# Splitting three of the four first w_ada groups, loading one whole group ahead of x, and scaling x's first blocks out of PSUM

## The reference

```python
sc = jax.nn.silu(c)                                   # c: 1 prompt row and 8 sampled rows
mod = sc @ w_ada + b_ada                              # 9 x 6144
sh1, s1, g1, sh2, s2, g2 = jnp.split(mod, 6, axis=-1)
h = rmsnorm(x, norm1_g) * (1 + s1) + sh1
z = h @ w_in                                          # 520 x 6144, then the three mixers, w_o, the experts
```

## Time and profile before

| | |
|---|---|
| median of three runs | 871.22 us (870.71 to 872.97) |
| the profiled execution | 873.34 us, of which the span of its instructions is 871.5 |
| TensorE matmul busy | 837.3 us, 96% of the span |
| VectorE busy | 686.0 us, 79% |
| ScalarE busy | 465.5 us, 53% |
| GpSimd busy | 77.0 us, 9% |
| mean granted TensorE clock | 0.988 |

### The profile page before, as it was taken

How to read it: one execution, slowest core, us unless ns; L and a number is a source line. 1 busy time by engine, 2 the same in 40 slices (tenths; PEclk the granted TensorE clock), 3 DMA queues, 4 the chain that set the end, 5 groups by cost and what they waited for, 6 DMA issues and landing times.

```text
span 871.5 us, 14885 instructions
## 1 busy us (share of the span) xinstructions
PE 837.3 (96%) x5035; PEld 699.3 (80%) x5035; DVE 686.0 (79%) x942; ACT 465.5 (53%) x556; POOL 77.0 (9%) x71
## 2 busy tenths in 40 slices
PE   7899999999999999999999889999999999999994
PEld 2589999989899999899777457888888888887851
DVE  0681638878798679599438879999989999899888
ACT  4552442343422221642222457888888888888852
POOL 0002000000000000230000001000100001003750
PEclk9889999999999999999999999999999999999998
DMA  9858545445443321123671579988896899999962
GB/s 329 276 166 277 200 126 170 138 151 164 148 152 118 97 80 66 55 74 123 237 251 73 175 275 390 393 313 317 312 400 219 322 398 400 400 399 397 359 196 98
DMA packets 90997, 201.24 MB, mean 231 GB/s; under 512 B 8792, under 2 KB 13400, under 8 KB 90918
## 3 DMA queue, kind: packets, MB, share of 16 engines
q1 hardware_dynamic: 78813, 165.25, 53.8%
q0 software_dynamic: 5136, 18.42, 6.0%
q10 hardware_dynamic: 7003, 16.95, 5.2%
HBM read 182.97 MB, written 18.35 MB: 231 GB/s over the span
## 4 chain that ended last, share of the span: by engine, by line
PE 81%; DVE 9%; DMA 3%; ACT 2%; issue 2%; SPq 1%; ACTq 1%; POOL 0%; POOLq 0%; DVEq 0%
PE ps L806 31%; PE ps L657 12%; PE ps L659 12%; PE ps L658 12%; PE ps L886 3%; DVE w_lo L1592 2%; PE ps L1001 2%; DMA region_a<-in_x_prompt_dram 2%; PE ps L1123 1%; PE ps L685 1%; PE ps L686 1%; PE ps L838 1%; ACT w_hi L1148 1%; DMA region_b<-h_rows,slot_idx 1%; PE ps L1036 1%
## 5 line engine op out<-in xcount | busy, mean ns | idle before, releaser
L1592 DVE TENSOR_TENSOR w_lo<-raw,w_hi 128x1024 fp32r<-128x1024 f32 x202 | 241.5, 1225 | 100.1 <-ACT w_hi L1148 98.3
L1148 ACT ACTIVATE w_hi<-raw 128x1024 fp32r<-128x1024 f32 x202 | 207.9, 1056 | 198.2 <-PE ps L806 150.6
L657 PE MATMUL ps<-w_hi,hT_hi 128*128 128x512 f32 (+1 forms) x512 | 205.6, 401 | 3.6 <-DVE w_lo L1592 1.4
L659 PE MATMUL ps<-w_hi,hT_lo 128*128 128x512 f32 (+1 forms) x512 | 202.1, 395 | 0.0
L658 PE MATMUL ps<-w_lo,hT_hi 128*128 128x512 f32 (+1 forms) x512 | 201.5, 393 | 0.0
L806 PE MATMUL ps<-hT_hi,w_hi 128*128 128x260 f32 x768 | 156.4, 285 | 1.9 <-ACT region_b L1242 1.1
L806 PE MATMUL ps<-hT_lo,w_hi 128*128 128x260 f32 x768 | 155.0, 283 | 0.0
L806 PE MATMUL ps<-hT_hi,w_lo 128*128 128x260 f32 x768 | 154.9, 283 | 0.0
L806 PEld LDWEIGHTS ps<-hT_hi,w_hi 128*128 128x128 f32 x768 | 118.8, 189 | 5.2 <-DVE w_lo L1592 3.9
L806 PEld LDWEIGHTS ps<-hT_lo,w_hi 128*128 128x128 f32 x768 | 119.4, 190 | 0.0
L806 PEld LDWEIGHTS ps<-hT_hi,w_lo 128*128 128x128 f32 x768 | 118.9, 189 | 0.0
(11 more groups left out here) (337 smaller groups left out, 838.6 us busy)
## 6 DMA issues: line engine op xcount, KB each, us to landing
raw<-in_exp_w_dram SPq DMA_DIRECT2D x96, 512.0 KB
region_a<-in_exp_w_dram SPq DMA_DIRECT2D x80, 512.0 KB
raw<-in_w_in_dram SPq DMA_DIRECT2D x48, 512.0 KB
raw<-in_w_ada_dram SPq DMA_DIRECT2D x30, 512.0 KB
expert_rows<-region_b ACTq DMA_DIRECT2D x17, 512.0 KB, 6.3
region_b<-in_exp_w_dram SPq DMA_DIRECT2D x16, 512.0 KB
region_b<-in_w_ada_dram SPq DMA_DIRECT2D x14, 512.0 KB, 8.1
expert_rows<-region_a POOLq DMA_DIRECT2D x8, 512.0 KB, 8.4
```

Of the source, the lines that this page charges most:

```text
L657: pe.matmul(out, pairs[0], moving[0], start=start, stop=False)
L659: return pe.matmul(out, pairs[1], moving[0], start=False, stop=stop)
L1148: act.activation(w_hi[:, split_slot(n), :], place, ACT.Copy).then_inc(hi_done, 1)
L1592: return dve.tensor_tensor(out, whole, first.bitcast(F32), ALU.subtract)
```

## The change

The first four w_ada groups are done as three split ones (0, 1 and 3) and one whole one (2); before, it was two and two. So twelve split quarters stand ahead of z 0 instead of eight (`N_HEAD`). SP loads group 0 (split quarters 0 to 3), the four whole quarters, then x, then the rest. TensorE starts with 32 identity transposes, products 0 to 3, the parameters, the four whole quarters, the turning of groups 0 and 2, and has more strings of identity transposes. ScalarE makes highs 0 to 3 and copies the whole group out before its squares of x, and scales x's tiles 2 and 3 itself. For blocks 0 to 3 of x ScalarE's copy to SBUF is gone: VectorE's `prompt_sum` reads PSUM, and ScalarE makes the high part from VectorE's sum. Blocks 4 to 7 go as before. All turning of mod now stands ahead of z 0. `z_quarter` becomes `z_part`, one call for each m, in the same order.

```diff
-G_NAT = 2
+G_WHOLE = 2
 G_HEAD = 4
 G_GAP = 2
-ITEMS = [("a", g) for g in range(G_NAT, G_HEAD)] + [("z", 0), ("z", 1)]
+HEAD_GROUPS = [g for g in range(G_HEAD) if g != G_WHOLE]
+ITEMS = [("a", g) for g in HEAD_GROUPS] + [("z", 0), ("z", 1)]
...
+N_NAT = 4
-N_HEAD = 4 * (G_HEAD - G_NAT)
+N_HEAD = 4 * len(HEAD_GROUPS)
+X_BANK = (2, 3, 6, 0, 2, 3, 6, 0)
...
@@ SP @@
-            for h in range(6):
-                native(h)
+            for n in range(4):
+                quarter(n)
+            for h in range(N_NAT):
+                sp.dma_start(native_place(h).rearrange("p (k n) -> p k n", k=2), ada_v[:, 2 * h:2 * h + 2, G_WHOLE * COLS:(G_WHOLE + 1) * COLS]).then_inc(nat_ready[h], 16)
             sp.dma_start(x_in[0:ND, 4, :], x_sample.rearrange("b t d -> (b t) d")).then_inc(x_landed[4], 16)
             for i in range(NP // P):
                 sp.dma_start(x_in[:, i, :], x_prompt[0, i * P:(i + 1) * P, :]).then_inc(x_landed[i], 16)
-            for h in range(6, 4 * G_NAT):
-                native(h)
-            for n in range(N_MIX):
+            for n in range(4, N_MIX):
...
@@ TensorE @@
-            pe.wait_ge(turned_out, 1)
-            for h in range(6):
-                native_quarter(h)
-            head_running(28)
-            for h in range(6, 4 * G_NAT):
-                native_quarter(h)
-            pe.wait_ge(xn_ready, NTILE)
-            for k in range(4):
-                turn_x(k, k)
-            pe.wait_ge(cT_split, 2)
-            ada_quarter(0, 4)
-            ada_quarter(1, 4)
-            for k in range(4, KD):
-                pe.wait_ge(xT_out, k - 3)
-                turn_x(k, k - 4)
-            ada_quarter(2, 4)
-            ada_quarter(3, 4)
-            pe.wait_ge(xT_out, KD)
-            turn_params()
-            ada_quarter(4, 7)
-            ada_quarter(5, 7)
-            pe.wait_ge(fold_ready, 1)
-            for g in range(3):
-                t = turn_mod(g, 0, 36 * g)
-            t.then_inc(modT_done, 1)
+            head_running(32)
+            pe.wait_ge(cT_split, 2)
+            for n in range(4):
+                ada_quarter(n, 4)
+            turn_params()
+            for h in range(N_NAT):
+                native_quarter(h)
+            pe.wait_ge(fold_ready, 1)
+            turn_mod(0, 1, 0)
+            head_running(8)
+            turn_mod(2, 1, 36).then_inc(modT_done, 1)
+            head_running(24)
+            for n in range(4, 6):
+                ada_quarter(n, 7)
+            pe.wait_ge(xn_ready, NTILE)
+            for k in range(2):
+                turn_x(k, X_BANK[k])
+            turn_sampled()
             ada_quarter(6, 7)
+            for k in range(2, 4):
+                turn_x(k, X_BANK[k])
             ada_quarter(7, 7)
+            for k in range(4, 6):
+                pe.wait_ge(hT_sum, k - 3)
+                turn_x(k, X_BANK[k])
+                ada_quarter(k + 4, 4)
+            for k in range(6, KD):
+                pe.wait_ge(hT_sum, k - 3)
+                turn_x(k, X_BANK[k])
+            ada_quarter(10, 4)
+            turn_mod(1, 7, 0)
+            ada_quarter(11, 4)
+            head_running(6, 1)
+            turn_mod(3, 7, 36).then_inc(modT_done, 1)
+            head_running(6, 1)
...
@@ ScalarE @@
-            native_out(0)
+            for n in range(4):
+                hi(n)
+            act.wait_ge(nat_used, N_NAT)
+            act.activation(mod[0:ND + 1, G_WHOLE * COLS:(G_WHOLE + 1) * COLS], ps[0:ND + 1, 5, :], ACT.Copy).then_inc(nat_out, 1)
             for n, i in enumerate((4, 0, 1, 2, 3)):
                 act.wait_ge(x_landed[i], 16)
...
             def input_prompt(k):
+                if k < 4:
+                    act.wait_ge(hT_sum, k + 1)
+                    act.activation(hT_hi[:, k, 0:NP], (tmp_a, tmp_b)[k % 2][:, 0:NP], ACT.Copy).then_inc(hT_hi_done, 1)
+                    return
...
+            for i in (2, 3):
+                act.wait_ge(x_rooted, 1)
+                act.activation(x_in[:, i, :], x_in[:, i, :], ACT.Copy, scale=sums[:, 3, i:i + 1]).then_inc(xn_ready, 1)
             hi(4)
             hi(5)
             input_sampled(0)
             input_prompt(0)
+            input_prompt(1)
+            hi(6)
+            input_prompt(2)
+            hi(7)
+            input_prompt(3)
             hi(8)
+            turned_x(4)
             hi(9)
+            for k in range(5, KD):
+                turned_x(k)
+            for n in range(10, 14):
+                hi(n)
             input_sampled(1)
...
@@ VectorE @@
+            for n in range(4):
+                lo(n)
+            mod_group(0)
+            params_out()
+            shift_out(0)
+            scale_out(0)
             mean_squares()
             norm_root()
-            for t in range(NTILE):
+            dve.wait_ge(shift_done, 1)
+            dve.sem_inc(x_rooted, 1)
+            for t in (4, 0, 1):
                 dve.tensor_scalar(x_in[0:rows(t), t, :], x_in[0:rows(t), t, :], sums[0:rows(t), 3, t:t + 1], None, ALU.mult).then_inc(xn_ready, 1)
+            lo(4)
             lo(5)
+            prompt_sum(0)
+            sampled_out()
             sampled_input(0)
+            prompt_sum(1)
             sampled_rest(0)
             prompt_rest(0)
+            lo(6)
+            prompt_rest(1)
+            prompt_sum(2)
+            lo(7)
+            mod_group(1)
+            prompt_sum(3)
+            prompt_rest(2)
             lo(8)
+            prompt_rest(3)
+            lo(9)
+            lo(10)
+            lo(11)
+            lo(12)
             mod_group(3)
+            shift_out(1)
             scale_out(1)
             sampled_input(1)
             prompt_sum(4)
             sampled_rest(1)
             prompt_rest(4)
+            lo(13)
...
```

More of the change, by code:

```diff
@@ L280, in trunk_step @@
         ld_x = sem("ld_x")
+        x_rooted = sem("x_rooted")
+        shift_done = sem("shift_done")
         x_landed = [sem(f"x_landed{i}") for i in range(NTILE)]
-        nat_ready = [sem(f"nat_ready{h}") for h in range(4 * G_NAT)]
+        nat_ready = [sem(f"nat_ready{h}") for h in range(4 * G_GAP)]
         apart_ready = [sem(f"apart_ready{n}") for n in range(N_APART)]
@@ L783, in z_quarter @@
                 hi, lo = split_weights(n, 2)
-                for m in range(4):
[L785 to L797, removed]
-                    for k in range(2):
-                        kk = 2 * q + k
-                        if g == 0 and m == 0:
-                            pe.wait_ge(hT_lo_done, kk + 2 + kk // 4)
-                        first, final = kk == 0, kk == KD - 1
-                        for w, x, start, stop in ((hi, hT_hi, first, False), (hi, hT_lo, False, False), (lo, hT_hi, False, final)):
-                            for h in range(2):
-                                mm = pe.matmul(ps[:, 2 * m + h, 0:HT], w[:, k, ms], x[:, kk, h * HT:(h + 1) * HT], start=start, stop=stop)
-                    if q == 3 and m < 3:
-                        mm.then_inc(z_done, 1)
@@ L810, in z_quarter @@
-                mm.then_inc(quarter_used, 1)
-            for i in range(G_HEAD - G_NAT, len(ITEMS)):
+                ms = slice(m * P, (m + 1) * P)
+                if q == 0:
+                    pe.wait_ge(set_free[m], g + 1)
+                    if m == 2 and ITEMS[n // 4 - 1][0] == "a":
+                        pe.wait_ge(mod_ready, SPLIT_GROUPS.index(ITEMS[n // 4 - 1][1]) + 1)
+                    elif m == 3 and g == 0:
+                        pe.wait_ge(scaleT_ready, 2)
+                for k in range(2):
+                    kk = 2 * q + k
+                    if g == 0 and m == 0:
+                        pe.wait_ge(hT_lo_done, kk + 2 + kk // 4)
+                    first, final = kk == 0, kk == KD - 1
+                    for w, x, start, stop in ((hi, hT_hi, first, False), (hi, hT_lo, False, False), (lo, hT_hi, False, final)):
+                        for h in range(2):
+                            mm = pe.matmul(ps[:, 2 * m + h, 0:HT], w[:, k, ms], x[:, kk, h * HT:(h + 1) * HT], start=start, stop=stop)
@@ L813, in _ @@
+                if m == 3:
+                    mm.then_inc(quarter_used, 1)
+                elif q == 3:
+                    mm.then_inc(z_done, 1)
+            pe.wait_ge(xT_out, KD // 2)
+            for q in range(4):
+                for m in range(4):
+                    z_part(0, q, m)
+            for i in range(len(HEAD_GROUPS) + 1, len(ITEMS)):
                 kind, g = ITEMS[i]
@@ L822, in _ @@
                     else:
-                        z_quarter(g, q)
+                        for m in range(4):
+                            z_part(g, q, m)
             unit = [0]
@@ L1212, in _ @@
                 input_prompt(k)
-            hi(10)
-            hi(11)
-            for n in range(N_HEAD + 4, N_HEAD + 7):
+            for n in range(N_HEAD + 2, N_HEAD + 7):
                 hi(n)
@@ L1227, in _ @@
             act.wait_ge(pads_ready, 1)
-            for i in range(G_HEAD - G_NAT, len(ITEMS)):
```

(7 more changed lines are left out.)

113 lines of the change are left out of this document (42 added, 71 removed).

## The result

The changed kernel takes 895.72 us (median of four runs, 894.07 to 897.57), the kernel before 870.97 (868.69 to 872.97). The ratio is 1.0279, 95% interval 1.0259 to 1.0298: slower by 2.8%. The forecast was 896.

What follows compares the result with a forecast made beforehand. TensorE's unedited z products were taken to bound the kernel, so z's start decides: +16.5 us at full clock, +29.6 at half, +25 taken on the 871.22 median, giving 896; range 882 to 904, 8 times in 10.

Steps and rivals of the forecast that it cites:

- part 1: Load order: x becomes the twelfth large load instead of the tenth, landing 2.7 us later at 23.5, first tile at 19.4.
- part 2: ScalarE's squares wait for the whole group's four native quarters; scaling starts at 31.7, x is scaled 7.0 us later.
- Steps (a) to (e): Chain from scaled x to the first z product, engines waiting in strict queue order: z at 66.8 (full clock) or 78.0 (half).
- half column: The chain from scaled x to z timed with TensorE at half clock, ending with z at 78.0; sum +29.6 us.
- Nine quarters, not seven: Between scaled x and the first z product, nine quarters (4 to 12) must be split, where before it was seven.
- PSUM sums: VectorE's sums reading PSUM: 0.6 us each taken, bounds 0.54 and 1.08; two on the chain, 0.0 to +1.1.
- part 4: Inside z group 0: the fold there is gone, gaining 2.8 us at full clock or 0.9 at half; the 1.1 of DMA issues stays.
- two thirds: Choice of a point between the full-clock sum, +16.5 us, and the half-clock sum, +29.6: +25 taken.
- clock up throughout: Rival: filling transposes and bursts hold TensorE's clock at full level, 888 us (884 to 891); chance 20%.
- The native group: Rival: TensorE does the whole group at half clock, 6.9 us becoming up to 13.8, total 903 (900 to 908); chance 10%.
- The shorter chain: Rival: some queue hand-offs between scaled x and z overlap better, three of about 3 us each, 880 (875 to 884); chance 10%.
- Faster: Rival: VectorE's own work, 18.1 us after scaled x, sets the start of z at 46.5, total 867; chance 6%.

Runs made afterwards that it cites:

- e5: The kernel before with all eight native quarters loaded ahead of x, nothing else edited: 874.11 us, 1.0031 of the kernel before.
- e1: The changed kernel with ScalarE's wait for the whole group and its copy-out moved to before the last of x's five squares: 891.27 us.
- e2: The changed kernel with highs and lows 4 to 7 ahead of everything that needs x's blocks: 884.89 us, z starting at 62.00.
- e8: e7 with blocks 4 to 7 turned earlier, highs 8 to 10 moved forward and 56 identity transposes in TensorE's waits: 871.17 us, z at 51.01.
- e3: The changed kernel with 188 more identity transposes in five TensorE waits to hold its clock: 887.44 us, z starting at 66.61.
- e10: The kernel before with 28 identity transposes in TensorE's waits to hold its clock: 869.67 us, 0.9974 of the kernel before.
- e7: The changed kernel with the edits of e1 and e2 together: 882.37 us, z starting at 60.99.
- e4: The changed kernel without the 32 identity transposes with which TensorE begins: 895.26 us, 1.0303 of the kernel before.

## Why the prediction was right

- **Loads (part 1).** x was to land at 23.5, its first tile at 19.4. In the changed kernel nothing waits for it, but the trace has its loads: the first is issued at 8.2 and takes 11.6 us to land (19.8), the last is issued at 9.6 and takes 14.0 (23.6). e5 measures what this costs in the kernel before, 2.7 us, the size predicted.
- **The squares behind the whole group (part 2), +7.0.** The native quarters start at 15.67 (16.3), end at about 22.7 (23.2), squares start at 23.24 (23.9), scaling at 31.05 (31.7), scaled at 33.2 (33.8). Each step was 0.5 to 0.7 late on paper, from the one estimate of low 3. Of the 7.6 us by which scaling is later than before, e1 takes 3.9 back by removing the wait and e5 gives 2.7 to x's later landing. The last 1.0 is the whole group's too: in e1 its eviction (0.57) still stands ahead of the last squares, and VectorE's shift and scale at 24.96, which need it, ahead of the mean.
- **Steps (a) to (e).** Low 6 ends at 45.75 (47.1 at half), low 7 at 52.3 (53.4), low 8 at 58.6 (59.3), low 10 at 66.2 (61.3 at full, 68.7 at half), z starts at 73.10 (66.8 and 78.0). Up to low 8 it went by the half column, 1.4 to 0.7 earlier, of which 0.6 is the earlier x; afterwards the clock was up for a while, 1.00 at 62 to 68 us, where the chain gained. e2 and e8 show that the hand-offs are the main cause, e3 that the clock is worth 6.5.
- **"Nine quarters, not seven".** This reading was wrong, though no term of the sum rests on it. In the kernel before, seven highs (2 to 8) come behind the scaling of x, but all nine lows (0 to 8) do, from 26.73 to 47.42 us, and nine (4 to 12) do in the changed kernel. The four quarters more are split ahead of x, so VectorE has no more splitting behind it than before, which fits what e8 takes back.
- **PSUM sums.** 0.80 instead of the 0.6 taken, inside the bounds of 0.54 and 1.08. By the Trainium skill, VectorE: DVE Perf Modes, Why PSUM operands drop a tier, the form gets its slowest mode there; 0.80 against 0.54 fits the direction.
- **In z (part 4), the step that was mis-sized.** I took 0.9 to 2.8 as gained, some 1.5 in the sum, and wrote that ScalarE's queue of DMA issues stays with its 1.1. z group 0 began at full clock, so all of the 2.8 came; and the 1.1 went too, since the issues of that queue took 4.4 us instead of 5.8 (the two `rbias` loads 0.60 and 0.45 instead of 1.30 and 1.22), which I hadn't expected. The two take 2.0 to 2.5 us in the profiled executions of the kernel before, e5 and e10, and 1.0 to 1.2 in the eleven others; why is open. So z starts 25.63 later and the five groups 21.47: 4.16 gained on the way.
- **The sum, and luck.** z was 1.2 earlier than the forecast's two thirds gives, and part 4 gave 2.6 more than its share, so the head and z 0 were oversized by 3.8 us: +21.5 at the five groups for +25.2. The profiled executions differ by 22.5 at the end, and 1.0 of that lies behind the five groups, where executions scatter over 3.4. The medians' +24.8 meets the +25 only by such scatter. That 896 was forecast and 895.72 measured is luck to the extent of 2 to 4 us; the mechanism is not.
- **The clock.** Two thirds of the way to the half-clock column was a choice; the first z product came at 73.10, where two thirds gives 74.3. The Trainium skill, TensorE: Matmul & The Clock Gate, HAM oscillation — how this bites in real kernels, says that a TensorE that waits between short bursts does each burst cold. The traces agree for 47 to 60 us (0.50), and e3 prices the half clock at 6.5 in all; but from 62 to 68 us TensorE waited 2.94 us and the clock stayed at 1.00.

The rivals: clock up throughout (888) is e3, measured at 887.4, and needs the strings. The native group wasn't done at half level. The shorter chain (880) didn't come by itself; it took the two edits of e7 (882.4). Faster (867) needed VectorE as the bound; e8 has that and gives 871, with z at 51.01 and not 46.5: behind the last low (48.5) an eviction, a fold and a string still follow one another, 2.5 us, which the 18.1 us of VectorE's work hadn't.

## What to carry to other kernels

In queues of strict order, list for each engine what stands in front of each instruction and doesn't need what it waits for: a weight's split behind a copy of x, or squares behind a product of other data, costs the whole wait, and the sign is a stretch in which no engine is busy for much more than half of the time and the DMA engines aren't either (a quarter to a third here). Price a head at both clock levels, and hold TensorE's clock with idle transposes wherever it waits, before judging an order: without it the second of two good edits (e7) moved the first main product by 1.0 us only. Compare with the old kernel at the same clock (e8 with e10). Follow a gain at several stations (first product, a later long stretch, the end), since 1 to 2 us don't show in the end.

## What the runs showed of the hardware

The granted clock doesn't follow TensorE's work at once. In the changed kernel it is 1.00 from 42 to 44 us with TensorE wholly idle, and 0.50 from 46 to 48 with TensorE busy throughout:

```profile
42.00:44.00 2.00, 0.00 (x0) 0.00 (x0) 1.66 (x4) 1.76 (x4) 0.00 (x0) 1.00 0.00 0
44.00:46.00 2.00, 0.21 (x1) 0.21 (x2) 1.49 (x2) 0.48 (x1) 0.00 (x0) 0.57 0.00 0
46.00:48.00 2.00, 2.00 (x7) 1.12 (x7) 0.34 (x1) 0.00 (x0) 0.00 (x0) 0.50 0.51 100
```

Ahead of the first change of level the column can't be trusted: e4 has 1.00 from 10 to 15 us, while its instructions come 0.43 apart as at half level. And strings of transposes of the identity hold it: with them a head that was at 0.50 for most of 26 us (e3; mean 0.57 from 34 to 60) or for 9 us (e10) stays at 1.00. ScalarE's high copy of a block that VectorE has just written takes 0.62 us, not the 0.55 that the prediction took.
